# Retention scores issued for two heads at a time, on the two row halves of the array

## What is computed

```python
h = rmsnorm(x, norm_g[l]) * (1.0 + scale) + shift
(a_q, a_f, a_i, a_g, b_cq, b_ckv, b_kr, b_g, c_q, c_k, c_v, c_g, m_a, m_b, m_c) = split_cols(h @ w_in[l])
...
y_c = retention_mixer(c_q, c_k, c_v, cos_r, sin_r) * silu(c_g)
merged = sigmoid(m_a) * (y_a @ w_pa[l]) + sigmoid(m_b) * (y_b @ w_pb[l]) + sigmoid(m_c) * (y_c @ w_pc[l])
x = x + gate * (merged @ w_out[l])
```

## Time and profile before

| | us |
|---|---|
| median of 3 runs | 1309.58 |
| lowest, highest | 1308.01, 1309.88 |
| profiled execution | 1307.09 |
| its span | 1305.30 |
| granted TensorE clock, mean | 0.997 |

### The profile page before, as it was taken

One profiled execution on the slowest core, in us unless ns is written; L12 is line 12 of the kernel. 1 busy time (PEld: TensorE's weight loads), 2 busy tenths in 40 slices (PEclk: granted clock), 3 DMA queues, 4 the chain that ended last, 5 costly groups with the idle time before them and its releaser, 6 DMA issues.

```text
span 1305.3 us, 16860 instructions
## 1 busy us (share of the span) xinstructions
PE 1273.2 (98%) x5772; PEld 1006.7 (77%) x5772; DVE 692.4 (53%) x1129; ACT 630.3 (48%) x958; POOL 719.2 (55%) x1470
## 2 busy tenths in 40 slices
PE   7999999999999999999999999999999999999996
PEld 4878887787678777788868888778876777778885
DVE  7677767634757234444365777553356533333332
ACT  5366656444553344444245666554455424344441
POOL 3365556774335554576645645576623474546662
PEclk9999999999999999999999999999999999999999
DMA  9432223342223433342222111223311232332331
GB/s 367 148 87 81 65 67 119 113 142 95 73 73 122 133 101 110 101 129 97 97 74 97 66 65 65 90 92 105 112 56 55 83 113 81 93 93 81 97 97 65
DMA packets 40902, 130.51 MB, mean 100 GB/s; under 512 B 5392, under 2 KB 5520, under 8 KB 39536
## 3 DMA queue, kind: packets, MB, share of 16 engines
q1 hardware_dynamic: 30448, 110.22, 25.8%
q10 hardware_dynamic: 10368, 19.21, 5.0%
HBM read 126.33 MB, written 2.10 MB: 98 GB/s over the span
## 4 chain that ended last, share of the span: by engine, by line
PE 89%; DVE 5%; ACT 2%; DMA 1%; POOL 1%; issue 1%; SPq 0%; DVEq 0%; ACTq 0%
PE ps_st L831 22%; PE ps_st L833 22%; PE ps_st L832 22%; PE ps_o L897 5%; PE ps_s L935 3%; PE ps_s L978 3%; PE ps_s L1001 2%; PE ps_misc L892 1%; PE ps_w L987 1%; DMA pro_w<-w_mod_first 1%; POOL w_lo L697 1%; ACT w_hi L1066 1%; PE ps_s L937 1%; PE ps_w L1013 0%; DVE sq_sum L1426 0%
## 5 line engine op out<-in xcount | busy, mean ns | idle before, releaser
L697 POOL TENSOR_TENSOR w_lo<-raw,w_hi 128x128 fp32r<-128x128 f32 x1448 | 708.4, 526 | 563.7 <-ACT w_hi L1066 563.6
L831 PE MATMUL ps_st<-h_hi,w_hi 128*128 128x512 f32 x920 | 372.7, 405 | 3.2 <-POOL w_lo L697 2.7
L833 PE MATMUL ps_st<-h_hi,w_lo 128*128 128x512 f32 x920 | 359.1, 390 | 0.0
L832 PE MATMUL ps_st<-h_lo,w_hi 128*128 128x512 f32 x920 | 358.6, 390 | 0.0
L1066 ACT ACTIVATE w_hi<-raw 128x1024 fp32r<-128x1024 f32 x182 | 190.5, 1047 | 70.9 <-PE ps_st L833 41.2
L831 PEld LDWEIGHTS ps_st<-h_hi,w_hi 128*128 128x128 f32 x920 | 172.9, 188 | 44.9 <-POOL w_lo L697 5.5
L832 PEld LDWEIGHTS ps_st<-h_lo,w_hi 128*128 128x128 f32 x920 | 173.0, 188 | 38.4 <-issue 4.8
L833 PEld LDWEIGHTS ps_st<-h_hi,w_lo 128*128 128x128 f32 x920 | 172.7, 188 | 36.9
L1388 DVE TENSOR_SCALAR gate_x<-ps_st 128x512 f32<-128x512 f32 x79 | 54.4, 689 | 198.2 <-PE ps_st L833 197.9
L1088 ACT ACTIVATE gate_t<-gate_x 128x512 f32<-128x512 f32 x80 | 50.5, 631 | 220.8 <-DVE gate_x L1388 219.9
L1090 ACT ACTIVATE gate_t<-gate_t,cs 128x512 f32<-128x512 f32 x80 | 57.9, 724 | 2.7
(11 more groups left out here) (317 smaller groups left out, 2028.5 us busy)
## 6 DMA issues: line engine op xcount, KB each, us to landing
raw<-w_stream SPq DMA_DIRECT2D x178, 512.0 KB, 3.5
mod_w<-w_mod ACTq DMA_DIRECT2D x64, 256.0 KB, 2.7
pro_w<-w_mod_first SPq DMA_DIRECT2D x8, 1024.0 KB, 16.0
x<-x_t SPq DMA_DIRECT2D x4, 512.0 KB, 7.4
ret_decay<-decay ACTq DMA_DIRECT2D x2, 1024.0 KB, 4.8
out_t<-o_t SPq DMA_DIRECT2D x8, 256.0 KB, 2.9
raw<-w_stream SPq DMA_DIRECT2D x4, 384.0 KB, 3.0
raw_extra<-w_stream SPq DMA_DIRECT2D x2, 512.0 KB, 19.9
```

The lines of the kernel that those rows point to most:

```text
L697: ins = nc.gpsimd.tensor_tensor(lo[:, r], whole[:, r], hi[:, r].bitcast(F32), ALU.subtract)
L831: nc.tensor.matmul(dst[0:m, :], wh, hi, start=(k == 0), stop=False)
L832: nc.tensor.matmul(dst[0:m, :], wh, lo, start=False, stop=False)
L833: last = nc.tensor.matmul(dst[0:m, :], wl, hi, start=False, stop=(k == nk - 1))
```

## The change

The list now takes the heads in pairs. For key block k it issues the scores of head h and of head h + 1 one behind the other, followed by one item (the items keep their order), for k = 0 to 3. Then come the value products of head h, an item, its `ret_out`, the item cg of head h + 1, the value products of head h + 1, an item, its `ret_out` (but for the last head, where it stands behind the last item, as before), an item. The two heads' scores go to the banks s0 (even head) and s1 (odd head). `ret_sc` exists twice, the second at 92 KB of the arena. VectorE's multiplies wait for the value products of the head two before, and only from the second pair on. The wait of the value products on score 2 is left out; score 3 is in the same bank. All other steps, operands and matmuls are as they were.

```diff
--- before.py
+++ after.py
@@ -213,16 +213,19 @@
         if it == ("rk", 1):
             s.append(("mla_lo", MLA_HEADS - 1))
     mb = merge_items("b")
-    for h in range(RET_HEADS):
-        s += [("ret_s", h, 0), ("ret_s", h, 1)]
-        item(*mb[3 * h])
-        s += [("ret_s", h, 2), ("ret_s", h, 3)]
-        item("cg", h)
-        s += [("ret_pv", h)]
-        item(*mb[3 * h + 1])
-        if h + 1 < RET_HEADS:
-            s.append(("ret_out", h))
-        item(*mb[3 * h + 2])
+    for h in range(0, RET_HEADS, 2):
+        for k, it in enumerate((mb[3 * h], ("cg", h), mb[3 * h + 1], mb[3 * h + 2])):
+            s += [("ret_s", h, k), ("ret_s", h + 1, k)]
+            item(*it)
+        s.append(("ret_pv", h))
+        item(*mb[3 * h + 3])
+        s.append(("ret_out", h))
+        item("cg", h + 1)
+        s.append(("ret_pv", h + 1))
+        item(*mb[3 * h + 4])
+        if h + 2 < RET_HEADS:
+            s.append(("ret_out", h + 1))
+        item(*mb[3 * h + 5])
     s.append(("ret_out", RET_HEADS - 1))
     for k, j in merge_items("c"):
         item(k, j)
@@ -297,7 +300,7 @@
         elif kind == "mla_pv":
             use("o", s)
         elif kind == "ret_s":
-            use(("s0", "s1")[s[2] % 2], s)
+            use(("s0", "s1")[s[1] % 2], s)
         elif kind == "mod_sum":
             use("w1", s)
     return uses, count
@@ -521,7 +524,7 @@
 
         ret_q, ret_k = at("ret_q", 0, [P, 2, SEQ]), at("ret_k", 4 * KB, [P, 2, SEQ])
         ret_v = at("ret_v", 8 * KB, [P, RET_HEADS, CH, P])
-        ret_sc = at("ret_sc", 16 * KB, [P, CH, SEQ])
+        ret_sc = at("ret_sc0", 16 * KB, [P, CH, SEQ]), at("ret_sc1", 92 * KB, [P, CH, SEQ])
         ret_decay = at("ret_decay", 24 * KB, [P, RET_HEADS, SEQ])
         yc_hi, yc_lo = at("yc_hi", 64 * KB, [P, CH, SEQ], F32R), at("yc_lo", 72 * KB, [P, CH, SEQ], F32R)
         ret_g = at("ret_g", 82 * KB, [P, SEQ])
@@ -1002,10 +1005,9 @@
                                               ret_q[r, h // 2, k * P:], start=True, stop=True), s)
                     elif kind == "ret_pv":
                         h = s[1]
-                        pe.wait_ge(free[e.bank_of(("ret_s", h, 2))], e.use(free, ("ret_s", h, 2)))
                         pe.wait_ge(free[e.bank_of(("ret_s", h, 3))], e.use(free, ("ret_s", h, 3)))
                         pe.wait_ge(free[RV_BANK[-1]], e.use(free, ("rv", CH - 1)))
-                        weighted_values(s, lambda k: ret_v[:, h, k, :], ret_sc)
+                        weighted_values(s, lambda k: ret_v[:, h, k, :], ret_sc[h % 2])
                     elif kind == "mod_sum":
                         pe.wait_ge(mod_done, e.at(mod_done, (s[1] + 1) * DT))
                         dst = take(s)
@@ -1824,9 +1826,9 @@
                         ps = bank[e.bank_of(s)]
                         if e.new(decay_in, 16):
                             dve.wait_ge(decay_in, e.at(decay_in, 16))
-                        if h >= 1:
-                            dve.wait_ge(full[e.bank_of(("ret_pv", h - 1))], e.use(full, ("ret_pv", h - 1)))
-                        V.tensor_tensor(ret_sc[:, k, k * P:], ps[:, 0:SEQ - k * P], ret_decay[:, h, 0:SEQ - k * P],
+                        if h >= 2:
+                            dve.wait_ge(full[e.bank_of(("ret_pv", h - 2))], e.use(full, ("ret_pv", h - 2)))
+                        V.tensor_tensor(ret_sc[h % 2][:, k, k * P:], ps[:, 0:SEQ - k * P], ret_decay[:, h, 0:SEQ - k * P],
                                         ALU.mult).then_inc(free[e.bank_of(s)], 1)
                         dve.wait_ge(free[e.bank_of(s)], e.use(free, s))
                     elif kind == "mod_acc":
```

## The result

| | before | changed |
|---|---|---|
| median, us | 1309.84 | 1303.45 |
| profiled execution | 1307.09 | 1301.37 |
| its span | 1305.30 | 1299.6 |
| granted clock, mean | 0.997 | 0.996 |

The ratio is 0.995, with a 95% interval of 0.9936 to 0.9964: 6.5 us faster (4.7 to 8.4). Five more rounds, in experiment 1, gave 0.994 (0.9921 to 0.9958). Single executions of the kernel before that took 1608.79 us here, and 2166.51 us beside experiments 5 and 6, are left out of the ratios. The direction was forecast, and the time lies in the range. But it isn't the mechanism of the forecast that stands in the profile, it is the rival "both passes overlap", which I had given 0.12.

A forecast was written before the change was run, and what follows sets the result against it. TensorE's gapless matmul stream was taken to bound the kernel. Overlapping one score record in four gave -4.3 us, all else 0, so the median would go from 1309.58 to 1305.3 us; range 1300.3 to 1311.0.

The forecast's parts named there:

- both passes overlap: Rival, score products: both records of head h run wholly beside those of head h + 1; 8.6 us, 1301.0 us; chance 0.12.
- What bounds the kernel: Both retention stretches: TensorE's matmul stream has no gap, so any gain must come out of that stream itself.
- A score product costs the same over 64 rows as over 128, plus 0.39 us a visit: Score products: 0.84 ns a column either way, plus 0.39 us for each visit to the 64-row form, in and out.
- As many visits as before, 0 us: Score runs in both layers: 16 visits before and after, 6.2 us paid both times, no difference.
- Two heads side by side: Score records A1, A2 (head h), B1, B2 (head h + 1): only B1 runs beside A2, one in four hidden; -4.3 us.
- Weights of the second half: Start of B1 in each visit: possible 0.10 us delay, 1.6 us in all, leaving 2.7; taken as nothing.
- VectorE, buffers, waits, order of value products and sums, w_lo: Work around the scores: decay multiplies, second score buffer, output bank release and weight loads stay covered; zero cost.
- The crossing as costly as a visit: Rival, between A2 and B1: changing halves costs 0.39 us, 16 times, without overlap; +6.2 us, 1315.8 us; chance 0.10.
- The sum against the median: Whole kernel: -4.3 us for the path and 0 for the rest, taking the median from 1309.58 to 1305.3 us.
- no overlap: Rival, score products: the halves run one after the other, only the order changes; 1309.6 us; chance 0.22.
- The range's own sum: Range over forecast, both passes and no overlap, with 0.8 us on either side for spread: 1300.3 to 1311.0.

The follow-up runs named there:

- experiment 1: The changed kernel once more with no edit, beside the kernel before: 1302.59 us, ratio 0.994.
- Experiment 5: The kernel before with score products over all 128 rows in place of 64, so each sums both heads of a pair: 1304.08 us, ratio 0.9953.
- experiment 6: The changed kernel with a product of 128 rows and 128 columns of constants between the two heads' scores in each visit: 1318.02 us, ratio 1.0059.
- experiment 2: The changed kernel with both heads of a pair on the same 64 rows, order and buffers kept: 1310.71 us, ratio 0.9998.
- experiment 4: The changed kernel with two key blocks in each visit, both of head h listed before both of head h + 1: 1297.72 us, ratio 0.9903.
- experiment 3: The changed kernel with two key blocks in each visit, heads h and h + 1 in turn: 1296.11 us, ratio 0.9893.

## Why the prediction was right or wrong

- **What bounds the kernel: right.** TensorE's stream had no gap in the two stretches, the change took 8.5 us out of that stream, and the span followed where the clock was the same (4.0 and 4.2 us in the two layers).
- **A score product costs the same over 64 rows as over 128, plus 0.39 us a visit: right.** Experiment 5 took the form away and got 0.39 us a visit and 6.2 us in all.
- **As many visits as before, 0 us: right.** The visit of experiment 2, with one half, has 2.56 - 0.46 - 4 x 0.43 = 0.38 us over its records, the changed kernel's with both halves 1.71 - 0.46 - 2 x 0.43 = 0.39.
- **Two heads side by side, -4.3 us: the step that failed.** I wrote: "If starts keep program order, B1 can start no sooner than A2, so B1 runs beside A2, and B2 waits for B1." Starts don't keep program order between the halves. B1 starts 7 ns after A1 and passes A2, and in experiment 4 it passes three records of A. With that, four record times become two and not three, and the term is 8.5 us. The sentence that I cited beside it from the Trainium skill, "TensorE: Matmul & The Clock Gate", section Part 3: Packing small matmuls — row/col tiling, was right that the halves work concurrently. What it says of the order of starts and ends doesn't hold for these products of two records each. In the changed kernel alone the products, taken whole, still begin and end in their order, 6 to 7 ns apart, and only their records interleave. It is experiment 4 that contradicts the order of whole products: B's first begins 0.95 us ahead of A's second, which the program lists before it. "TensorEngine Tiling (Array Packing)", section Theoretical Speedup, with its factor of up to 2, is what the record times show: 2 x 0.43 us in place of 4 x 0.43. My error of weighing was to let an assumption that no row supported carry 0.52, and the other one 0.12, when the rows spoke for neither.
- **Weights of the second half, 0 to 1.6 us: right at 0.** The record behind the first pair comes after 0.53 us, as before, and this is paid once for both halves.
- **VectorE, buffers, waits, order of value products and sums, w_lo: right at 0.** TensorE is busy without a gap in both stretches after the change as well. The bank was released within 0.1 us of the estimate.
- **The crossing as costly as a visit: excluded.** Changing the half costs nothing that can be measured; a full-height product in the same place (experiment 6) does cost it.
- **The sum against the median.** By 8.5 us the median should have come to 1301.1. It came to 1303.45 and 1302.59. The mechanism isn't short: at equal clock the spans are 8.4 us apart, and in experiment 1, where 17 executions of the kernel before and 6 of the changed one have the same mean clock (0.994), the medians are 8.3 us apart. The first six of the changed kernel got 0.991 twice, 0.994 three times and 0.996 once; the clocks of the kernel before in those rounds are not listed, so that this explains all of the remaining 2 us there is likely and not shown. The forecast's 1305.3 missed by 1.9 us; the error of mechanism was 4.2 us, and luck covered half of it. That the range held says little of the mechanism, since it took in both passes and no overlap as well.
- **The range's own sum: wrong, without effect.** It was to add 0.8 us on either side; 1300.3 is 0.7 below the 1301.0 of both passes, but 1311.0 is 1.4 above the 1309.6 of no overlap.

## What to carry to other kernels

Products with a contraction of 64 belong in pairs on the two row halves, with no full-height product between them: the records of a pair then take the time of one product's, also in fp32 with its two records for each product. All pairs here wrote to different banks; one bank for both wasn't tried. What lies around them counts as much: a visit to the 64-row form costs 0.39 us for going in and out together, so collect several such products in one visit. Four were tried, in two orders, and the order made no difference. Where an overlap isn't shown in the trace of before, give both queue rules their own time, and weigh them equally until a row decides.

## What the runs showed of the hardware that I had not expected

- In the 64-row form records of one half pass records of the other that the program lists earlier: the first record of B starts 7 ns after the first of A with one product of A ahead of it, 14 ns with two. With a full-height product between them it started 1.47 us after (experiment 6).
- Records of the two halves run side by side at full speed: in experiment 3 the second pair of records of 512 columns starts at 440.77 and the next pair at 441.20, 0.43 us later, as for a record alone.
- With nothing changed in the beginning of the kernel, the granted clock between 20 and 40 us was 0.91 in some profiles and 0.74 in others, and the same kernel's first scores moved between 442.25 and 443.99. Over a whole execution, the same kernel's spans followed the mean granted clock: 1302.8 to 1303.5 us at 0.991 and 1297.9 to 1299.6 at 0.996. Differences of 2 us in this kernel should be read between two marks inside the trace, not from its span.
